# A decoder trunk on one Trainium2 core: two output projection units share one PSUM region inside the last pair of heads

## The chip, the core and the metric

The kernel runs on one core of a Trainium2 chip. The engines of a core work at the same time and wait for each other by semaphores: TensorE (matmuls, PE in the profile; PEld is its loading of weights), VectorE (DVE), ScalarE (ACT), GpSimd (POOL) and SyncE (SP), which here only issues DMAs. The metric is the device time of one launch in microseconds.

## The reference

A step of a decoder trunk with two layers, D = 1024, in float32. A prompt of 1024 tokens and 8 sequences of 4 sample tokens go through it with shared weights.

```python
for layer in range(2):
    xn = rms_norm(h, g_mix[layer])
    if layer == 0:  y = conv_mixers(xn)          # projection, two gated convolutions, output projection
    else:                                        # 16 heads of 64
        q, k, v = qkv_split(xn, w_qkv)
        y = dilated_attention(q, k, v) @ w_o     # three dilated windows, merged; cache for the samples
    h = h + y
    h = h + conv_ffn(rms_norm(h, g_ffn[layer]))  # gate and up, convolution of width 3, silu, down
y = rms_norm(h, g_final)
```

The change touches the product with `w_o` of layer 1: the attention output (1056 tokens by 1024 channels) times a matrix of 1024 by 1024, added to h. Results are y, the new convolution states and the new key and value caches.

## The kernel before, in words

**Layout.** Activations are held transposed: 128 channels on the partitions, the 1056 tokens (1024 of the prompt, 32 samples) along the row, eight such rows of a tile for 1024 channels. A matmul takes 352 tokens, so three make a row. To keep float32 accuracy each operand is split into a high and a low part: `w_sp` holds both parts of a weight unit, `xs` those of the activations. A product is made of three: high by high, high by low, low by high. One weight unit (128 by 1024 numbers, 512 KB) gives 128 output channels. It has eight parts, one for each row of 128 input channels, and a part is 3 x 3 = 9 matmuls.

**Weight stream.** Units follow each other through three slots: SyncE loads into `w_raw` (`load_unit`), ScalarE writes the high part (`split_hi`, line 375), GpSimd the low part (`split_lo`, line 380, counted in `w_lo`). Units 118 to 125 are the output projection (`U_WO` = 118).

**PSUM.** Two regions `reg[0]` and `reg[1]` of three banks, and `ob` of two. Outside attention, units go into the regions in turn. `open_use` lets TensorE write a region once VectorE has emptied it, and `add_to_h` (line 1505) adds a finished region to a row of h. In the attention `reg[1]` holds scores and transposes, and `reg[0]` (`dense`) the projections that run as filling.

**Attention.** The 16 heads are taken in eight pairs. A pair has eight steps s, one for each block of 128 queries, the longest first: step 0 has eight key blocks, step 7 has one. A step's scores go through PSUM to VectorE (adding of the bias and minimum, `neg_scores`, line 1801), ScalarE (exponential), VectorE (normalising, line 1817), TensorE (transposes, `turn`, line 900), copies to `pT` by VectorE (line 1824, head 0) and ScalarE (line 1255, head 1), and TensorE (`weigh`, line 915, probabilities by values). Steps 0 to 3 have more than four key blocks: there `turn(s, 0)` is followed by a second set, `turn(s, 4)`. In steps 0, 1, 3, 5 and 7 a phase of the samples' attention is put in (`sample_phase`), for which SyncE loads the cached keys and values into `kvr`.

**Filling.** TensorE's order is written out by hand. `filler(n)` has 24 places in a pair, n = 0 to 23. In step s, place 3s + 1 stands ahead of the next step's scores and of `turn(s, 0)`, and place 3s + 2 behind `turn(s, 0)` (in step 7 ahead of it). In pairs 0 to 6 each place takes one part of the next pair's q, k or v unit (line 879). In the last pair there is no next one; there places 4, 7, 10, 13, 16, 19 and 22 take parts 0 to 6 of unit 118 (`in_proj`, line 612). A part k needs row k of the attention output split: ScalarE's high part (`att_hi`, line 1260; two rows at the end of steps 0, 1 and 2, one in step 3) and GpSimd's low part (line 1453, counted in `x_lo`). Row 7 is that of the last pair itself; ScalarE and VectorE make it behind the pair (lines 1337 and 1903).

**Behind the pairs.** TensorE waits for the copies of the last samples' output, then runs parts 0 to 6 of unit 119 in region 1, part 7 of unit 118, part 7 of unit 119, and then units 120 to 125. So 81 matmuls stand ahead of unit 120. SyncE loads rows 0 to 2 of h back from HBM once the last sample phase is through (h and `kvr` share memory, line 560), then unit 120 once the last pair's sample output is copied, then rows 3 to 7 (line 566), the FFN state and unit 121. Unit 120's slot shares memory with tiles of the attention, so its load is not earlier.

`VT` is the tile of the pair's value rows before they are turned, 1056 numbers per partition. After its transposes at the start of the pair and its store to HBM it is not used any more in the last pair. The kernel's addresses show that it does not overlap h.

Of the kernel before, what the change touches and what calls it, by code (L numbers as in the profile page):

```python
# [24 lines left out]
ALU = mybir.AluOpType  # L25
# [3 lines left out]
P = 128  # L29
D = 1024  # L30
KD = D // P
# [3 lines left out]
NT, TS = 3, T // 3  # L35
# [7 lines left out]
NPAIR = NH // 2  # L43
# [91 lines left out]
NTA = _n + 1  # L135

KV_LEN = (512, NKEY - 512)

SQ0 = {0: 0, "ln": 8, 1: 12, 2: 20, 3: 28, 4: 36}

# [6 lines left out]
def cnt(u):  # L147

    return u + 1 if u < U_WO else u + 1 - QKV_LATER
# [24 lines left out]
def build(nc, xT, wstream, par, ident_d, ones_d, stA, stB, stF, kva, kvb, wtab, sbias, cache_k, cache_v,  # L174
# [3 lines left out]
    with ExitStack() as ctx:  # L178
# [4 lines left out]
        def sem(name):  # L183
            return ctx.enter_context(nc.semaphore(name))
# [89 lines left out]
        def region(use):  # L274
            return reg[use % 2][:, :, 0:TS]

        def tok(ap):
            return ap.rearrange("p (s t) -> p s t", s=NT)
# [41 lines left out]
        ta_full, ta_free, tb_full, tb_free = (sem(s) for s in ("ta_full", "ta_free", "tb_full", "tb_free"))  # L320
        pv_ok, o_free = sem("pv_ok"), sem("o_free")
        seam_ok = sem("seam_ok")
        sp_neg, sp_exp, sp_ok, so_ok, zero_ok = (sem(s) for s in ("sp_neg", "sp_exp", "sp_ok", "so_ok", "zero_ok"))
        v_chain, a_chain, g_chain = sem("v_chain"), sem("a_chain"), sem("g_chain")

# [264 lines left out]
        def _(pe):  # L590
# [5 lines left out]
            def in_proj(u, r, i=None, ustep=12, rstep=24, x_at=None, order=range(KD), part=range(KD), midway=None,  # L596
                        released=0):


                pe.wait_ge(w_lo, at(cnt(u), i, ustep))  # L600
                open_use(r, i, rstep)
                out = region(r)
                w = w_sp[:, u % 3]
                for n in part:
                    k = order[n]
                    if midway and n == KD // 2:
                        midway()
                    if x_at is not None:
                        pe.wait_ge(x_lo, x_at + n + 1)
                    for wh, xh in ((0, 0), (0, 1), (1, 0)):  # L610
                        for t in range(NT):
                            mm = nc.tensor.matmul(out[:, t, :], w[:, wh, k * P:(k + 1) * P],  # L612
                                                  xs[:, xh, k, t * TS:(t + 1) * TS],
                                                  start=(n == 0 and wh + xh == 0), stop=(n == KD - 1 and wh == 1))
                    if n < released:
                        mm.then_inc(x_free, 1)
                if KD - 1 in part:
                    mm.then_inc(full, 1)
# [233 lines left out]
            def scores(pr, s, c):  # L852
# [7 lines left out]
                                          KT[pr.par][rows, lo:lo + w], start=True, stop=True)  # L860
                mm.then_inc(sc_full, 1)

            def pair(pr):
                k_t = KT[pr.par]

                def filler(n):

                    if pr.last:
                        if n % 3 == 1 and n > 1:
                            in_proj(U_WO, R1, x_at=4 * KD, part=(n // 3 - 1,))  # L870
                        return
                    x, k = divmod(n, KD)
                    if k == 0:
                        pe.wait_ge(aw_lo, pr.n(x + 1, 3))
                        pe.wait_ge(d_free, pr.n(x + 3, 3))
                    w = w_sp[:, pr.slot(x)]
                    for wh, xh in ((0, 0), (0, 1), (1, 0)):
                        for t in range(NT):
                            mm = nc.tensor.matmul(dense[:, t, :], w[:, wh, k * P:(k + 1) * P],  # L879
                                                  xs[:, xh, k, t * TS:(t + 1) * TS],  # L880
                                                  start=(k == 0 and wh + xh == 0), stop=(k == KD - 1 and wh == 1))
                    if k == KD - 1:
                        mm.then_inc(d_full, 1)
# [134 lines left out]
            pairs(pair)  # L1018

            pe.wait_ge(ta_free, NTA * NPAIR + 1)  # L1020
            in_proj(U_WO + 1, FIRST[U_WO + 1], part=range(KD - 1))
            in_proj(U_WO, FIRST[U_WO], x_at=4 * KD, part=(KD - 1,))
            in_proj(U_WO + 1, FIRST[U_WO + 1], part=(KD - 1,))
            for m in range(2, KD - 2):
                in_proj(U_WO + m, FIRST[U_WO + m])
            last_two(U_WO + KD - 2, FIRST[U_WO + KD - 2])
# [439 lines left out]
        def _(dve):  # L1466
# [342 lines left out]
            def pair(pr):  # L1809
# [31 lines left out]
                for s in range(STEPS):  # L1841
# [12 lines left out]
                    if s == 2 and not pr.last:  # L1854
                        dve.wait_ge(d_full, pr.n(4, 3))
                        project(0, dense, QT[1 - pr.par])
                    if s == 4:
                        dve.wait_ge(sp_exp, pr.n(1, 1))
                        chain(nc.vector.reciprocal(snm[:, 4:5], snm[:, 3:4]))
                        nc.vector.tensor_scalar(sps[:, :], sps[:, :], snm[:, 4:5], None, ALU.mult).then_inc(sp_ok, 1)  # L1860
# [44 lines left out]
            dve.wait_ge(o_free, 2 * NPAIR + 1)  # L1905
            chain(nc.vector.memset(g3[:, 0:PAD], 0.0))
            dve.wait_ge(h_back, 16 * 3)
            for m in range(KD):
                if m == 3:
                    dve.wait_ge(h_rest, 16 * (KD - 3))  # L1910
                if m == KD - 2:
                    for x in range(KD - 2):
                        gain_lo(3, 5, x)
                add_to_h(FIRST[U_WO + m], m)
# [171 lines left out]
```

## Time and profile before

| what | value |
|---|---|
| median of 3 runs | 2684.63 us (2684.56 to 2685.1) |
| profiled execution, its own time | 2685.45 us |
| its span | 2683.6 us |
| TensorE busy | 2629.0 us, 98% |
| VectorE / ScalarE / GpSimd busy | 1392.3 / 626.4 / 683.0 us |
| the chain that ended last | TensorE 93%, VectorE 4%, ScalarE 1% |

The span is what the profiler saw from the first to the last instruction; the time of the execution holds a little more around it. Busy time of matmuls overlaps with the loading of their weights. The chain of waits is followed back from the last instruction: each link is the work that the next one waited for. In the views of busy time by stage a row gives the stretch from the span's start and its length, then the busy time of TensorE, its loading of weights, VectorE, ScalarE and GpSimd, each with the number of instructions, then TensorE's granted clock (1.00 is full speed), the mean busy share of the DMA engines and what they moved in GB/s. In a timeline, brackets give how long the engine sat idle before the row and what ended that. All rows below lie between 1659 and 1835 us of the span: pair 6 begins its scores near 1659, the last pair runs from 1736.5 to 1805.7, and the output projection follows.

### The profile page before, as it was taken

Reading aid. Unit: us, or ns where it says so; the run is one execution under the profiler, and the core shown is the slowest. Engines: PE = TensorE matmul, PEld = TensorE weight load, DVE = VectorE, ACT = ScalarE, POOL = GpSimd, SP = SyncE. Lnnn points to the kernel's source line nnn. Section 1 sums busy time; section 2 is a strip of 40 time slices with the busy share of each in tenths; the row PEclk is TensorE's granted clock in tenths of the full one; section 3 lists DMA queues with packets and bytes.
Section 4 is the critical chain, followed back from the end, with each engine's and each line's share of the span. In section 5 each row is a group of like instructions: output and inputs, shape, how many; then the busy total and the mean of one; then the engine's idle time right before and its main releaser. Section 6 shows DMA issues by size and latency. Waiting matters only on the chain.

```text
span 2683.6 us, 41415 instructions
## 1 busy us (share of the span) xinstructions
PE 2629.0 (98%) x17588; PEld 2468.5 (92%) x17588; DVE 1392.3 (52%) x2030; ACT 626.4 (23%) x940; POOL 683.0 (25%) x397
## 2 busy tenths in 40 slices
PE   8999999999999999999999999989999999999997
PEld 8889999999999999997777777769999999999997
DVE  6989855444444444465655555561544444444444
ACT  5110342111111111143333333342311111111112
POOL 1001143332223223340101101124432333323332
PEclk9999999999999999999999999999999999999998
DMA  4101112243333344144444354437444444444411
GB/s 140 48 32 40 48 45 54 63 149 110 110 110 104 108 142 140 50 153 138 145 142 167 133 173 142 163 126 288 166 172 157 157 157 152 169 172 173 172 44 65
DMA packets 93864, 336.72 MB, mean 125 GB/s; under 512 B 22528, under 2 KB 39808, under 8 KB 91136
## 3 DMA queue, kind: packets, MB, share of 16 engines
q1 hardware_dynamic: 93696, 334.20, 36.1%
q8 instruction: 139, 2.28, 0.4%
q14 instruction: 29, 0.24, 0.0%
HBM read 315.88 MB, written 152.25 MB: 174 GB/s over the span
## 4 chain that ended last, share of the span: by engine, by line
PE 93%; DVE 4%; ACT 1%; issue 1%; DMA 0%; POOL 0%; POOLq 0%; DVEq 0%; SPq 0%; ACTq 0%
PE reg L612 49%; PE reg L663 19%; PE reg L879 9%; PE reg L859 3%; PE reg L751 3%; PE ob L915 3%; PE reg L900 1%; PE reg L832 1%; PE ob L725 1%; PE ob L900 1%; PE reg L968 1%; PE reg L632 1%; PE reg L955 1%; DVE neg_s L1801 1%; DVE neg_s L1817 1%
## 5 line engine op out<-in xcount | busy, mean ns | idle before, releaser
L612 PE MATMUL reg<-xs,w_sp 128*128 128x352 f32 x8208 | 1338.7, 324 | 12.1 <-DVE xs L1494 11.7
L612 PEld LDWEIGHTS reg<-xs,w_sp 128*128 128x128 f32 x8208 | 1329.3, 188 | 17.3 <-issue 16.7
L380 POOL TENSOR_TENSOR w_sp<-w_raw,w_sp 128x1024 fp32r<-128x1024 f32 x152 | 370.3, 2436 | 985.4 <-ACT w_sp L375 984.1
L663 PE MATMUL reg<-hid,w_sp 128*128 128x352 f32 x3150 | 511.5, 323 | 0.0
L663 PEld LDWEIGHTS reg<-hid,w_sp 128*128 128x128 f32 x3150 | 508.5, 188 | 0.2 <-DVE tmp L1739 0.2
L375 ACT ACTIVATE w_sp<-w_raw 128x1024 fp32r<-128x1024 f32 x172 | 182.2, 1059 | 1102.8 <-PE reg L612 668.8
L1505 DVE TENSOR_TENSOR h<-reg,h 128x1056 f32<-128x1056 f32 x199 | 250.1, 1257 | 290.5 <-PE reg L663 233.0
L879 PE MATMUL reg<-xs,w_sp 128*128 128x352 f32 x1512 | 279.6, 332 | 0.0
L1705 DVE TENSOR_TENSOR g<-reg,rst 128x1056 f32<-128x1056 f32 x44 | 55.4, 1259 | 415.1 <-PE reg L612 415.1
L879 PEld LDWEIGHTS reg<-xs,w_sp 128*128 128x128 f32 x1512 | 240.6, 188 | 17.7 <-issue 17.6
L398 POOL TENSOR_TENSOR w_sp<-w_raw,w_sp 128x1024 fp32r<-128x1024 f32 x21 | 49.9, 2376 | 477.2 <-ACT w_sp L393 457.9
L1421 POOL TENSOR_TENSOR sil<-sil,rst 128x1056 f32<-128x1056 f32 x44 | 90.4, 2054 | 218.0 <-ACT sil L1192 218.0
L1739 DVE TENSOR_TENSOR tmp<-reg,sil 128x1056 f32<-128x1056 f32 x44 | 55.3, 1257 | 151.2 <-POOL sil L1421 79.6
L1192 ACT ACTIVATE sil<-acc 128x1056 f32<-128x1056 f32 x44 | 47.9, 1089 | 342.9 <-DVE acc L1730 342.9
L1255 ACT ACTIVATE pT<-ob 128x512 f32<-128x512 f32 (+1 forms) x96 | 47.1, 491 | 329.3 <-PE ob L900 329.3
L1718 DVE SCALAR_TENSOR_TENSOR acc<-g,pt,acc 128x1024 f32<-128x1024 f32 x88 | 113.0, 1284 | 12.0 <-DVE acc L1716 1.5
L1801 DVE CUSTOM_DVE_ANT_0 neg_s<-reg,wt 128x512 f32<-128x512 f32 (+1 forms) x192 | 107.2, 558 | 6.6
L1248 ACT ACTIVATE neg_s<-neg_s,nmx 128x896 f32<-128x896 f32 (+7 forms) x128 | 98.1, 768 | 36.8 <-DVE nmx L1806 34.2
L1548 DVE SCALAR_TENSOR_TENSOR g<-g,pt,g 128x1024 f32<-128x1024 f32 x75 | 103.4, 1379 | 2.0
L1824 DVE COPY pT<-reg 128x512 f32<-128x512 f32 (+1 forms) x96 | 53.3, 556 | 97.9 <-PE reg L900 97.5
L1694 DVE TENSOR_TENSOR hid<-tmp,hid 128x1056 fp32r<-128x1056 f32 x44 | 100.3, 2280 | 2.3 <-ACT hid L1195 2.3
L751 PE MATMUL reg<-xs,w_sp 128*128 128x352 f32 x576 | 96.9, 328 | 1.0 <-DVE xs L1501 0.7
(207 smaller groups left out, 1951.7 us busy)
## 6 DMA issues: line engine op xcount, KB each, us to landing
w_raw<-in_wstream SPq DMA_DIRECT2D x193, 512.0 KB, 3.6
out_sv<-in_cache_v SPq DMA_DIRECT2D x16, 4088.0 KB, 15.4
out_sk<-in_cache_k SPq DMA_DIRECT2D x16, 4088.0 KB, 15.1
kvr<-in_kva SPq DMA_DIRECT2D x16, 2048.0 KB, 9.4
kvr<-in_kvb SPq DMA_DIRECT2D x16, 1536.0 KB, 7.0
wt<-in_wtab SPq DMA_DIRECT2D x16, 512.0 KB, 5.6
h<-in_xT SPq DMA_DIRECT2D x4, 1056.0 KB, 11.2
h_spill<-h SPq DMA_DIRECT2D x8, 528.0 KB, 2.6
```

The source lines that it names most:

```text
L375: nc.scalar.activation(w_sp[:, u % 3, 0, :], w_raw[:, u % 3, :], ACT.Copy).then_inc(w_hi, 1)
L380: nc.gpsimd.tensor_tensor(w_sp[:, u % 3, 1, :], w_raw[:, u % 3, :], w_sp[:, u % 3, 0, :].bitcast(F32), ALU.subtract).then_inc(w_lo, 1)
L612: mm = nc.tensor.matmul(out[:, t, :], w[:, wh, k * P:(k + 1) * P], xs[:, xh, k, t * TS:(t + 1) * TS], start=(n == 0 and wh + xh == 0), sto ...
L663: mm = nc.tensor.matmul(out[:, t, :], w[:, wh, kk * 512 + m * P:kk * 512 + (m + 1) * P], hid[:, par_g, kk, xh, t * TS:(t + 1) * TS], start ...
L751: mm = nc.tensor.matmul(out[:, t, :], w[:, wh, (2 * k + m2) * P:(2 * k + m2 + 1) * P], xs[:, xh, place + k, t * TS:(t + 1) * TS], start=(k ...
L879: mm = nc.tensor.matmul(dense[:, t, :], w[:, wh, k * P:(k + 1) * P], xs[:, xh, k, t * TS:(t + 1) * TS], start=(k == 0 and wh + xh == 0), s ...
L1248: nc.scalar.activation(neg_s[:, hh, 0:w], neg_s[:, hh, 0:w], ACT.Exp, bias=nmx[:, m, hh:hh + 1], scale=-1.0, accum_out=lsum[:, 0, hh:hh + ...
L1505: nc.vector.tensor_tensor(tok(h[:, m, :]), region(r), tok(h[:, m, :]), ALU.add).then_inc(free, 1)
L1548: ins = nc.vector.scalar_tensor_tensor(out=y, in0=src, scalar=w, in1=y, op0=ALU.mult, op1=ALU.add)
L1694: nc.vector.tensor_tensor(hid[:, g % 2, c, 1, :], tmp[:, :], hid[:, g % 2, c, 0, :].bitcast(F32), ALU.subtract).then_inc(hid_lo, 1)
L1718: chain(nc.vector.scalar_tensor_tensor(out=y, in0=src, scalar=w, in1=y, op0=ALU.mult, op1=ALU.add))
L1801: nc.vector.tensor_tensor_reduce(out=neg_s[:, hh, lo:lo + w], in0=S[hh][:, 0:w], in1=wt[:, hh, t0:t0 + w], scale=-1.0, scalar=3.0e38, op0= ...
```

## The change

In the last pair the filling now holds twelve parts. Places 4, 5, 7, 8, 10, 11 and 13 take parts 0 to 6 of unit 119 (`part_proj`), into `dense`. VectorE copies that partial sum of seven parts to `VT` in step 4, behind the normalising and ahead of the rescaling of the samples' probabilities. Places 14, 16, 17, 19 and 20 then take parts 0 to 4 of unit 118 into the same region; the first of them waits for the copy. Places 2 and 22 are empty.

Behind the pairs TensorE runs parts 5 to 7 of unit 118, and part 7 of unit 119 alone in region 1: 36 matmuls ahead of unit 120. VectorE adds `VT` to row 1 of h ahead of its first `add_to_h`. What SyncE, ScalarE and GpSimd issue is the same as before and in the same order.

```diff
--- before.py
+++ after.py
@@ -135,6 +135,9 @@
 NTA = _n + 1
 
 KV_LEN = (512, NKEY - 512)
+
+WO_PART = {n: k for k, n in enumerate((4, 5, 7, 8, 10, 11, 13))}
+WO_REST = {n: k for k, n in enumerate((14, 16, 17, 19, 20))}
 
 SQ0 = {0: 0, "ln": 8, 1: 12, 2: 20, 3: 28, 4: 36}
 
@@ -320,6 +323,7 @@
         ta_full, ta_free, tb_full, tb_free = (sem(s) for s in ("ta_full", "ta_free", "tb_full", "tb_free"))
         pv_ok, o_free = sem("pv_ok"), sem("o_free")
         seam_ok = sem("seam_ok")
+        part_full, part_out, part_in = (sem(s) for s in ("part_full", "part_out", "part_in"))
         sp_neg, sp_exp, sp_ok, so_ok, zero_ok = (sem(s) for s in ("sp_neg", "sp_exp", "sp_ok", "so_ok", "zero_ok"))
         v_chain, a_chain, g_chain = sem("v_chain"), sem("a_chain"), sem("g_chain")
 
@@ -860,14 +864,31 @@
                                           KT[pr.par][rows, lo:lo + w], start=True, stop=True)
                 mm.then_inc(sc_full, 1)
 
+            def part_proj(k):
+
+                pe.wait_ge(w_lo, cnt(U_WO + 1))
+                pe.wait_ge(x_lo, 4 * KD + k + 1)
+                w = w_sp[:, (U_WO + 1) % 3]
+                for wh, xh in ((0, 0), (0, 1), (1, 0)):
+                    for t in range(NT):
+                        mm = nc.tensor.matmul(dense[:, t, :], w[:, wh, k * P:(k + 1) * P],
+                                              xs[:, xh, k, t * TS:(t + 1) * TS],
+                                              start=(k == 0 and wh + xh == 0), stop=(k == KD - 2 and wh == 1))
+                if k == KD - 2:
+                    mm.then_inc(part_full, 1)
+
             def pair(pr):
                 k_t = KT[pr.par]
 
                 def filler(n):
 
                     if pr.last:
-                        if n % 3 == 1 and n > 1:
-                            in_proj(U_WO, R1, x_at=4 * KD, part=(n // 3 - 1,))
+                        if n in WO_PART:
+                            part_proj(WO_PART[n])
+                        elif n in WO_REST:
+                            if WO_REST[n] == 0:
+                                pe.wait_ge(part_out, 1)
+                            in_proj(U_WO, R1, x_at=4 * KD, part=(WO_REST[n],))
                         return
                     x, k = divmod(n, KD)
                     if k == 0:
@@ -1018,9 +1039,14 @@
             pairs(pair)
 
             pe.wait_ge(ta_free, NTA * NPAIR + 1)
-            in_proj(U_WO + 1, FIRST[U_WO + 1], part=range(KD - 1))
-            in_proj(U_WO, FIRST[U_WO], x_at=4 * KD, part=(KD - 1,))
-            in_proj(U_WO + 1, FIRST[U_WO + 1], part=(KD - 1,))
+            in_proj(U_WO, FIRST[U_WO], x_at=4 * KD, part=range(len(WO_REST), KD))
+            u = U_WO + 1
+            open_use(FIRST[u])
+            for wh, xh in ((0, 0), (0, 1), (1, 0)):
+                for t in range(NT):
+                    mm = nc.tensor.matmul(region(FIRST[u])[:, t, :], w_sp[:, u % 3, wh, (KD - 1) * P:KD * P],
+                                          xs[:, xh, KD - 1, t * TS:(t + 1) * TS], start=(wh + xh == 0), stop=(wh == 1))
+            mm.then_inc(full, 1)
             for m in range(2, KD - 2):
                 in_proj(U_WO + m, FIRST[U_WO + m])
             last_two(U_WO + KD - 2, FIRST[U_WO + KD - 2])
@@ -1854,6 +1880,10 @@
                     if s == 2 and not pr.last:
                         dve.wait_ge(d_full, pr.n(4, 3))
                         project(0, dense, QT[1 - pr.par])
+                    if s == 4 and pr.last:
+                        dve.wait_ge(part_full, 1)
+                        dve.wait_ge(vt_out, 16 * NPAIR)
+                        nc.vector.tensor_copy(tok(VT[:, :]), dense).then_inc(part_out, 1)
                     if s == 4:
                         dve.wait_ge(sp_exp, pr.n(1, 1))
                         chain(nc.vector.reciprocal(snm[:, 4:5], snm[:, 3:4]))
@@ -1905,6 +1935,9 @@
             dve.wait_ge(o_free, 2 * NPAIR + 1)
             chain(nc.vector.memset(g3[:, 0:PAD], 0.0))
             dve.wait_ge(h_back, 16 * 3)
+            dve.wait_ge(part_out, 1)
+            nc.vector.tensor_tensor(h[:, 1, :], VT[:, :], h[:, 1, :], ALU.add).then_inc(part_in, 1)
+            dve.wait_ge(part_in, 1)
             for m in range(KD):
                 if m == 3:
                     dve.wait_ge(h_rest, 16 * (KD - 3))
```

## Rows read from the trace of the kernel before

**Rows 1.** Busy time by stage: pair 6, then the last pair with its tail.

```profile
1659.08:1736.50 77.42, 76.26 (x663) 59.52 (x663) 44.07 (x140) 26.53 (x66) 7.12 (x3) 1.00 0.43 149
1736.50:1807.00 70.50, 57.15 (x524) 38.20 (x525) 46.46 (x139) 32.58 (x70) 20.29 (x8) 0.98 0.38 131
```

**Rows 2.** Chain of waits from the last pair on: start us, us, what.

```profile
1759.22 0.49 ACT pT L1255
1759.71 1.94 ACT xs L1260 x2
...
1763.74 2.60 DVE neg_s L1817
...
1802.08 0.35 PE reg L974 x8
...
1805.67 11.94 PE reg L612 x72
...
1819.21 30.81 PE reg L612 x189
```

**Rows 3.** Timeline of GpSimd: start us, us, line, operation, count, idle before.

```profile
1760.76 5.15 POOL L1453 TENSOR_TENSOR xs<-att,xs 128x1056 fp32r<-128x1056 f32 x2 [6.29 <-ACT xs L1260]
...
1781.38 2.45 POOL L1453 TENSOR_TENSOR xs<-att,xs 128x1056 fp32r<-128x1056 f32 x1 [6.67 <-ACT xs L1260]
1812.49 2.40 POOL L380 TENSOR_TENSOR w_sp<-w_raw,w_sp 128x1024 fp32r<-128x1024 f32 x1 [28.66 <-ACT w_sp L375]
```

**Rows 4.** Timeline of TensorE in the last pair, steps 1, 4, 5 and 6.

```profile
1757.35 0.60 PE L900 MATMUL ob<-ident,neg_s 128*128 128x128 f32 x4
1758.29 0.55 PE L900 MATMUL reg<-ident,neg_s 128*128 128x128 f32 x3 [0.35 <-DVE pT L1824]
...
1781.31 1.74 PE L612 MATMUL reg<-xs,w_sp 128*128 128x352 f32 x9
...
1786.69 1.09 PE L915 MATMUL ob<-pT,vrow 128*64 128x128 f32 x16 [1.27 <-ACT att L1267]
...
1789.67 1.95 PE L968 MATMUL reg<-kvr,spT 128*32 128x128 f32 x64 [0.86 <-ACT spT L1284]
...
1795.37 0.88 PE L915 MATMUL ob<-pT,vrow 128*64 128x128 f32 x12 [0.67 <-ACT pT L1255]
...
1799.49 0.66 PE L915 MATMUL ob<-pT,vrow 128*64 128x128 f32 x8 [0.56 <-ACT pT L1255]
```

**Rows 5.** Timeline of ScalarE: a row's conversion, and two splits of weights.

```profile
1780.23 1.07 ACT L1260 ACTIVATE xs<-att 128x1056 fp32r<-128x1056 f32 x1
...
1811.35 1.06 ACT L375 ACTIVATE w_sp<-w_raw 128x1024 fp32r<-128x1024 f32 x1 [3.99 <-DMA w_raw<-in_wstream]
1819.49 1.06 ACT L375 ACTIVATE w_sp<-w_raw 128x1024 fp32r<-128x1024 f32 x1 [7.08 <-DMA w_raw<-in_wstream]
```

**Rows 6.** Timeline of VectorE: copies of two sizes, and a subtraction.

```profile
1757.55 0.69 DVE L1824 COPY pT<-reg 128x512 f32<-128x512 f32 x1 [1.81 <-PE reg L900]
...
1804.23 0.29 DVE L1824 COPY pT<-reg 128x128 f32<-128x128 f32 x1 [1.31 <-PE reg L900]
1807.39 1.26 DVE L1903 TENSOR_TENSOR xs<-att,xs 128x1056 fp32r<-128x1056 f32 x1 [2.88 <-ACT xs L1337]
```

**Rows 7.** Timeline of SyncE's queue: issues, not landings.

```profile
1737.80 0.34 SPq L526 DMA_DIRECT2D out_vT<-VT  x1
...
1802.54 1.29 SPq L560 DMA_DIRECT2D h<-h_spill  x3
1805.65 0.33 SPq L368 DMA_DIRECT2D w_raw<-in_wstream  x1
```

**Rows 8.** The loads of h from line 560, issue to landing.

```profile
DMA to landing us min/median/max: 3.8/4.7/5.5
```

**Rows 9.** Busy time, granted clock and DMA, columns as in rows 1.

```profile
1769.00:1773.00 4.00, 4.00 (x40) 2.78 (x42) 2.73 (x13) 3.15 (x6) 3.37 (x2) 0.57 0.00 0
1807.00:1811.00 4.00, 4.00 (x27) 4.00 (x26) 1.30 (x2) 0.36 (x1) 0.00 (x0) 1.00 1.03 415
```


## The prediction

> **What bounds the kernel now.** TensorE is the bound nearly everywhere, so I first compared two stretches in the view of busy time by stage. The reader is to see there that pair 6 takes 77.42 us with TensorE busy for 76.26 us, while the last pair (1736.50 to 1807.00) takes 70.50 us with TensorE busy for only 57.15 us [rows 1]. So 13.35 us of TensorE time lie idle in the last pair, and that is what more filling could use. Then I read the chain of waits of the last pair. It shows whether this idle time is free. It is mostly not: between two steps the chain runs from the second set of transposes of a step to ScalarE's copy of them (1759.22), to two conversions of attention rows (1759.71, 1.94 us), and on to VectorE's normalising, whose second instruction takes 2.60 us (1763.74) [rows 2]. GpSimd shows why that one is so long: its two subtractions run from 1760.76 to 1765.91, and VectorE ends 0.43 us behind them [rows 2, 3]. So the idle gaps of TensorE are links of a chain that TensorE itself starts; what delays the transposes delays all of it. Last I read what follows the pair: 81 matmuls without a pause (72 of them 11.94 us, so a part of nine costs 1.49 us), one addition by VectorE, and from 1819.21 the third projection unit, whose matmuls then run on unbroken [rows 2].
>
> **The change part by part.**
>
> *Moved work.* The number of projection matmuls stays the same. The last pair had seven parts and gets twelve; behind the pair nine parts become four. Behind the pair 5 x 1.49 = 7.5 us leave TensorE's queue. Inside it, six parts are added between the transposes of a step and what comes next (numbers 5, 8, 11, 14, 17, 20), and the one at number 22 goes. Number 22 stood behind the last sample phase, so up to the end of that phase, which I call S (1802.45 before, where the matmuls that start at 1802.08 end [rows 2]), six parts are added. What decides is how late S becomes.
>
> *Steps 1 to 3.* Here the new part stands between the first and the second set of transposes. In step 1 the first set is through at 1757.9, the second started at 1758.29 after an idle 0.35 us [rows 4]. Now it starts at about 1759.4: +1.1. Everything behind it in the chain, the conversions, GpSimd's subtractions and the normalising that ends with them, moves as much. In step 2 the idle time ahead of the second set is near nothing, and the part ahead of the scores (number 7) now needs row 2, which GpSimd has ready 2.6 us after it starts (half of 5.15 us, 1760.76) [rows 3]; this wait ends as late as the normalising lets the transposes go anyway and adds 0.1 to 0.2. Step 2: +1.25. Step 3 has the same idle time of 0.35 us ahead of its second set (there are two such rows): +1.15. Together +3.5 us by ScalarE's copy at the end of step 3. These are between 0 (all in idle time) and 1.5 each; I take the sum of the single steps because the chain names every link.
>
> *Step 4.* The part at number 13 was the fourth one and needed a row long done; it becomes the seventh and needs row 6. ScalarE makes it at 1780.23 and GpSimd subtracts from 1781.38 for 2.45 us, to 1783.83 [rows 3, 5], while TensorE is ready for the part at 1781.31 [rows 4]. With the +3.5 on the rows and +2.4 on TensorE, TensorE waits some 3.5 us, and the part ends at 1788.8. Scores and transposes are behind it in TensorE's queue, and they end at 1790.8, 5.5 us later than before. VectorE's new copy (1056 columns from PSUM; a copy of 512 takes 0.69 us, one of 128 some 0.29, so about 1.26 us by the slope, and not under 0.69) stands ahead of the sample rescaling, of the transposes' copy and of the next scores, which all wait for it [rows 6]. It ends at 1790.2, so the other unit can open the region without a wait at number 14. That part takes 1.5 us of a gap of 1.27 us (1786.69) [rows 4], and the sample's transposes and their copies come 5.7 us later than before (1789.67, where TensorE waited 0.86 us) [rows 4]. The wait for the values' store costs nothing: it was issued at 1737.80, some 50 us earlier [rows 7].
>
> *Steps 5 and 6.* The new part falls into the gaps of 0.67 us and 0.56 us ahead of the weighing (1795.37 and 1799.49) [rows 4]: +0.85 and +0.95. S comes 7.5 us late, about 1810.0. All six parts are 9.0 us, so only 1.5 us of them lie in idle time, or rather in that and in what the two stalls leave. Lower bound +1 (all but one part hidden), upper +10.
>
> *Behind S.* Before, the third unit started at S + 16.76. Now TensorE has transposes, the last weighing and four parts, 36 matmuls or 6.0 us: without the part at number 22 it gets to the four parts at S + 1.9 (before at S + 3.2), and is through at S + 8.0. The last row's conversion ends on VectorE some 3.0 us after the end of the weighing, since ScalarE's copies and the 1.26 us subtraction (1807.39) follow each other [rows 6]; the first two parts (2.98 us) just cover it. The new addition of the stored sum (two inputs in SBUF, as the subtraction of 1.26 us [rows 6]) needs rows of h that were asked for at S + 0.1 and landed within 5.5 us of each issue [rows 7, 8], that is by S + 6.5, and is done at S + 7.7. It delays the first addition by 1.2 us but not TensorE, for what comes next is later.
>
> *The new wait.* The third unit's weights are not moved by the change. SyncE issued their load at 1805.65, once the pair had ended, behind three loads of h; they landed by 1811.35, ScalarE took 1.06 us and GpSimd 2.40 us from 1812.49, so that they were ready at 1814.89, S + 12.45 [rows 3, 5, 7]. Before, 4.3 us of matmuls still lay over this. Now TensorE is done at S + 8.0 and stands for some 4.2 us. The load is issued 1.3 us earlier against S; but its queue is full (DMA share 1.03, 415 GB/s) [rows 9], and three times 528 KB lie ahead, so between 0 and 1.3 us of it come through; I take 0.3, near the full queue.
>
> *The sum.* S +7.5; start of the third unit S + 12.15 instead of S + 16.76, so -4.6; together +2.9, rounded to +3.0 us. Behind that nothing changes: the next weights landed at about S + 17 (1819.49) and their split ends 3.5 us later, at about S + 20.6 [rows 5], while TensorE wants them at S + 12.15 + 11.8 = S + 24; the rest of h is wanted later still. The profiled execution took 2685.45 us, its span 2683.6 us; so 2688.5 us for such an execution, and since the median of the runs is 0.8 us lower, 2687.6 us.
>
> **The rivals.**
>
> *A, the clock falls in the new waits.* The trace shows it once: from 1769 to 1773 the granted clock was 0.57 in the mean, so nearly all of it at the 1.2 GHz level (0.5), after a stretch in which TensorE often paused; in before it lay beside VectorE's work and cost nothing [rows 9]. Over full matmuls such a dip costs 4 x (1 - 0.57) = 1.7 us. The change makes two longer pauses, 3.5 us in step 4 and 4.2 us ahead of the third unit; with a dip behind each, +6.4 us, 2691.0 us, which is slower. It decides from the point where both dips come, or one and a longer S. Against it: the mean clock of the last pair is 0.98 with all its gaps of up to 1.3 us [rows 1, 4], and more filling makes the pair denser. The Trainium skill (TensorE: Matmul & The Clock Gate, Part 1) has a rule that speaks against this change: the clock is cut after a stretch without activity and comes back only after a busy one. By that rule both dips are likely; the trace neither shows nor excludes it for such lengths.
>
> *B, the parts fit the gaps.* The idle 13.35 us are more than the 9.0 us added [rows 1]. If the steps' gaps give way, S comes only 2 us late (the stall in step 4), and the sum is 2 - 4.6 = -2.6: 2682.0 us. For it: pair 6 runs 24 parts in 77.42 us. Against it: pair 6 has no conversions of rows, and the chain of the last pair names ScalarE and VectorE right behind the transposes [rows 2]. Break-even is S at +4.6.
>
> *C, the change does all it can.* Parts hidden and weights there in time: -7.5 us, 2677.1 us. It needs the load earlier than it is issued; nothing moves it.
>
> **How the numbers follow.** Forecast 62%, A 18%, B 17%, C 3%. Two thirds of A reach past 0.2% (5.4 us, about what a measurement of this kernel can tell from no change), of B hardly anything, C all: faster 4%, slower 12%, same 84%. The range reaches from B's nearer half to just past A's value: 2682.5 to 2691.5 us.
>
> **What would show it.** Right: in the chain the transposes of steps 1 to 3 come 1.1 to 1.3 us later per step; the seventh part waits for GpSimd's seventh subtraction; the last sample phase ends about 7.5 us later; ahead of the third unit TensorE waits about 4 us for GpSimd's split. Wrong: if S moves by under 4.6 us, or if that last wait is under 2 us, the sign is wrong. A granted clock of 0.5 in the first part of the third unit would be rival A.

## The result, and the profile after

The changed kernel took 2689.31 us (median of 19 runs, 2688.58 to 2691.65), the kernel before 2685.04 us (19 runs, 2683.83 to 2688.23) beside it. The ratio is 1.0017, with a 95% interval of 1.0011 to 1.0023: 4.6 us slower, 3.0 to 6.2 (the medians alone differ by 4.3). The forecast was 3.0 us slower. The profiled execution has a span of 2687.6 us, 4.0 more than before.

Single spans differ by more than a microsecond in stretches that no kernel here changes: the last pair began 1.12 us earlier than in the profile of before (1735.28 instead of 1736.40). So I measure from T, the start of the last pair's first scores (1736.40 before), to S, the end of its last sample phase, from S to the start of unit 120, and the length of the first four units from there (288 matmuls). This table holds all profiles, in us; each value is a difference of starts and ends in the chain of waits and in TensorE's timeline. "By profile" is the sum against that of before; "by runs" is the difference of the medians, each kernel against before in the same comparison. The two differ by up to 2 us, for one profile is one execution.

| kernel | T to S | S to unit 120 | four units | sum | by profile | by runs |
|---|---|---|---|---|---|---|
| before | 66.03 | 16.78 | 46.84 | 129.65 | | |
| after | 75.17 | 11.43 | 48.39 | 134.99 | +5.3 | +4.3 |
| e1_early_load | 75.12 | 9.63 | 46.84 | 131.59 | +1.9 | +1.2 |
| e2_before_early_load | 66.03 | 16.77 | 46.84 | 129.64 | 0.0 | +0.3 |
| e3_warm | 73.62 | 11.28 | 46.88 | 131.78 | +2.1 | +3.7 |
| e4_row_ready | 72.64 | 11.16 | 49.59 | 133.39 | +3.7 | +3.2 |
| e5_more_early | 69.58 | 16.76 | 46.84 | 133.18 | +3.5 | +3.7 |
| e6_more_late | 67.56 | 16.75 | 46.84 | 131.15 | +1.5 | +2.5 |
| e7_six | 70.04 | 11.40 | 49.47 | 130.91 | +1.3 | +2.2 |
| e8_six_early | 69.94 | 8.27 | 46.84 | 125.05 | -4.6 | -2.7 |
| e9_two_in_step1 | 69.53 | 8.27 | 46.84 | 124.64 | -5.0 | -3.6 |
| e10_six_early_again | 70.04 | 8.25 | 46.84 | 125.13 | -4.5 | -2.6 |

The forecast's terms were 73.5, 12.15 and 46.84. The first came 1.7 us too long, the second 0.7 us better, the third 1.55 us too long.

The view of busy time by stage, columns as in [rows 1], for pair 6 and for the last pair of the changed kernel:

```profile
1659.00:1735.40 76.40, 75.24 (x661) 59.27 (x661) 43.11 (x141) 26.54 (x66) 7.14 (x3) 1.00 0.42 148
1735.40:1812.00 76.60, 63.03 (x561) 45.34 (x561) 48.11 (x140) 30.84 (x67) 20.27 (x8) 0.96 0.32 106
```

TensorE stands idle for 13.6 us of the last row, as much as the 13.35 before: old gaps were filled, but new waits arose, and the pair became longer. (The stretch of [rows 1] ended 1.3 us into the matmuls behind the pair, this one 0.3 us ahead of them; the idle time is not touched by that.) The mean granted clock is 0.96, where it was 0.98.

The chain of waits (start, length, what) answers to [rows 2]:

```profile
1758.99 0.49 ACT pT L1281
...
1760.53 2.44 POOL xs L1479
...
1763.10 1.68 PE reg L874 x9
...
1768.78 0.38 ACT pT L1281
...
1781.86 0.28 ACT pT L1281
...
1784.23 2.42 POOL xs L1479
...
1786.78 1.92 PE reg L874 x9
...
1810.10 0.40 PE reg L995 x8
...
1812.27 6.06 DMA w_raw<-in_wstream
...
1818.35 1.06 ACT w_sp L379
...
1819.49 2.36 POOL w_sp L384
...
1821.88 28.16 PE reg L616 x163
```

In it the reader sees three things. In step 2 and in step 4 the chain runs through GpSimd's subtraction (1760.53 and 1784.23) into a part of the projection (1763.10 and 1786.78): TensorE waits for a row of attention. And ahead of unit 120 (1821.88) it runs over a DMA, ScalarE and GpSimd; before, 72 matmuls stood in that place.

TensorE's timeline, with the idle time in brackets, answers to [rows 4]:

```profile
1756.58 1.71 PE L874 MATMUL reg<-xs,w_sp 128*128 128x352 f32 x9
1758.13 0.49 PE L921 MATMUL reg<-ident,neg_s 128*128 128x128 f32 x3
...
1786.78 1.92 PE L874 MATMUL reg<-xs,w_sp 128*128 128x352 f32 x9 [3.19 <-POOL xs L1479]
...
1791.64 1.70 PE L616 MATMUL reg<-xs,w_sp 128*128 128x352 f32 x9
...
1793.28 1.09 PE L936 MATMUL ob<-pT,vrow 128*64 128x128 f32 x16
...
1796.17 1.95 PE L989 MATMUL reg<-kvr,spT 128*32 128x128 f32 x64 [0.78 <-ACT spT L1310]
...
1802.60 0.88 PE L936 MATMUL ob<-pT,vrow 128*64 128x128 f32 x12
...
1807.51 0.66 PE L936 MATMUL ob<-pT,vrow 128*64 128x128 f32 x8
```

The new part at 1756.58 used up the 0.35 us ahead of the second transposes and pushed them by 1.0 us against T. Part 13 waits 3.19 us (1786.78). The gaps of 1.27, 0.67 and 0.56 us ahead of the weighing are gone (1793.28, 1802.60, 1807.51). The 0.78 us ahead of the sample's values (1796.17) stayed.

VectorE's timeline shows the new copy, what stands behind it, and the new addition:

```profile
1788.74 1.26 DVE L1886 COPY VT<-reg 128x1056 f32<-128x1056 f32 x1 [1.23 <-PE reg L874]
...
1791.37 0.69 DVE L1850 COPY pT<-reg 128x512 f32<-128x512 f32 x1 [0.56 <-PE reg L921]
...
1817.16 1.26 DVE L1939 TENSOR_TENSOR h<-VT,h 128x1056 f32<-128x1056 f32 x1 [1.84 <-issue]
1818.45 2.62 DVE L1531 TENSOR_TENSOR h<-reg,h 128x1056 f32<-128x1056 f32 x2
```

The copy took 1.26 us, as the slope had it. The transposes' copy at 1791.37 then waited 0.56 us for TensorE, so the new copy was not what ended last there. SyncE's queue, to be held against [rows 7]:

```profile
1810.57 1.29 SPq L564 DMA_DIRECT2D h<-h_spill  x3
1812.27 0.33 SPq L372 DMA_DIRECT2D w_raw<-in_wstream  x1
```

The load of unit 120's weights is issued 1.70 us behind the loads of h, and not 3.11 us. It landed by 1818.35, S + 7.9, where before it was S + 8.9.

Last the granted clock, the figure ahead of the last two in each row, in the steps 3 and 4 and at the start of unit 120:

```profile
1776.00:1780.00 4.00, 3.59 (x16) 2.83 (x17) 1.96 (x6) 0.60 (x1) 0.00 (x0) 0.72 0.98 367
1780.00:1784.00 4.00, 3.13 (x29) 2.67 (x27) 1.13 (x6) 2.14 (x4) 0.00 (x0) 0.85 0.06 19
1784.00:1788.00 4.00, 1.22 (x8) 1.25 (x9) 2.49 (x4) 1.56 (x5) 2.41 (x1) 1.00 0.00 0
1788.00:1792.00 4.00, 4.00 (x17) 2.54 (x17) 2.66 (x5) 0.07 (x1) 0.00 (x0) 0.57 0.00 0
1822.00:1825.00 3.00, 3.00 (x11) 3.00 (x12) 0.00 (x0) 0.00 (x0) 0.00 (x0) 0.53 1.03 416
1825.00:1828.00 3.00, 3.00 (x18) 3.00 (x18) 0.00 (x0) 1.43 (x2) 0.30 (x1) 0.90 1.42 600
```

A dip is a stretch in which the granted clock lies near 0.5, the 1.2 GHz level. Three dips lie over work that counts: one in step 3 (the first two rows), one in step 4 from 1788 on, behind the wait of part 13, and one at the very start of unit 120. The last is what made the four units 1.55 us longer. The one in step 4 can be sized by the time from the start of part 13 to the start of the part at place 14: 4.86 us here (1786.78 to 1791.64), and 3.56 us at full clock (e8_six_early, shown with that experiment), so about 1.3 us, an estimate. The one in step 3 is sized with e3_warm.

### The profile page after: what moved, and what is told of

It is laid out like the page before. It is cut to its first block, busy times and chain, and to the rows that moved or that the text cites. A ratio compares the mean times of both kernels' runs of the same rounds, so it can differ in the third digit from the quotient of the medians.

```text
span 2687.6 us, 41423 instructions
## 1 busy us (share of the span) xinstructions
PE 2629.2 (98%) x17588; PEld 2469.8 (92%) x17588; DVE 1395.5 (52%) x2032; ACT 626.1 (23%) x940; POOL 683.0 (25%) x397
## 4 chain that ended last, share of the span: by engine, by line
PE 93%; DVE 4%; issue 1%; ACT 1%; DMA 0%; POOL 0%; POOLq 0%; DVEq 0%; SPq 0%; ACTq 0%
PE reg L616 49%; PE reg L667 19%; PE reg L900 9%; PE reg L863 3%; PE reg L755 3%; PE ob L936 2%; PE reg L921 1%; PE reg L836 1%; PE ob L729 1%; PE ob L921 1%; PE reg L989 1%; PE reg L636 1%; PE reg L976 1%; DVE neg_s L1827 1%; DVE neg_s L1843 1%
```

## The experiments

All twelve profiles are read against their own T. The ratios are those of the runs, each with its 95% interval; five rounds resolve about 2.4 us either way, so the steps are told apart by the profiles, and the runs say whether the whole follows.

**The weights of unit 120 earlier.** In the changed kernel (e1_early_load) and in the kernel before (e2_before_early_load) the load is issued in step 4 of the last pair, into half of the bias table that nobody reads from there on; the splits read it from there, and the FFN state, which shares that memory, is loaded behind the split.

```diff
                 if not pr.last:
                     sp.wait_ge(sc_free, pr.n(2 * CHUNK0[4] + 1, 2 * NCH))
                     load_table(0, wtab[0][pr.p + 1])
+                else:
+                    sp.wait_ge(sc_free, pr.n(2 * CHUNK0[4] + 1, 2 * NCH))
+                    sp.dma_start(wt[:, :, 0:512], wstream[U_WO + 2]...).then_inc(w_in[(U_WO + 2) % 3], 16)
...
-            load_unit(sp, U_WO + 2, (U_WO + 2) % 3)
```

> The changed kernel with the weights of unit 120 loaded during step 4 of the last pair, into the first half of the bias table, which is free from there on; nothing is left out. My theory: TensorE's wait of 3.4 us for these weights goes; what is late next is VectorE's addition to h (the stored sum is added first, up to S + 7.9, then unit 118's region is emptied at about S + 9.3), so unit 120 starts some 2 us earlier against S, and the clock dip behind the wait (1.55 us) goes too: 3.5 us faster than the changed kernel, about +0.8 us against before. Rival 'it is all the longer pair' (the wait only takes up slack): no change, +4.3 us against before. Rival 'the wait is all of it': -0.5 us against before or less.

Measured: ratio 1.0003 (0.9994 to 1.0012), 2685.76 us where before took 2684.58: +1.2 us by the medians. The wait for the weights is gone, the four units are back at 46.84 us, and what stands ahead of unit 120 is VectorE's addition of the stored sum and the first addition behind it, as expected. VectorE's timeline, then TensorE's:

```profile
1816.36 1.54 DVE L1948 TENSOR_TENSOR h<-VT,h 128x1056 f32<-128x1056 f32 x1 [1.79 <-issue]
```

```profile
1819.34 15.92 PE L620 MATMUL reg<-xs,w_sp 128*128 128x352 f32 x97 [1.60 <-DVE h L1540]
```

Unit 120 waits 1.60 us for VectorE, and no dip follows that shorter pause. The sum in the profiles fell by 3.4 us (expected 3.5).

> The kernel before with the same earlier load of unit 120; nothing is left out. My theory: there 81 matmuls cover the load and its split, so it gives nothing: within 0.3 us of before. A rival in which the queue behind the load (rows of h, unit 121) matters would show 1 us or more, faster.

Measured: ratio 0.9999 (0.9990 to 1.0008), and in the profile every term as before. The load was covered there. The two runs together show that the changed kernel made the wait, by moving the matmuls that had hidden it.

**Work in the wait.** e3_warm keeps the changed kernel and puts 20 matmuls that nobody reads into the wait.

```diff
             mm.then_inc(full, 1)
+            for t in range(20):
+                nc.tensor.matmul(ob[:, 0, 0:TS], xs[:, 0, KD - 1, 0:P], xs[:, 0, KD - 1, 0:TS], start=True, stop=True)
             for m in range(2, KD - 2):
```

> The changed kernel with 20 matmuls of 352 columns that nobody reads, put into the wait ahead of unit 120 (some 3.3 us of the 3.4 us). My theory: the granted clock falls to the 1.2 GHz level in the first part of unit 120 because TensorE stood still ahead of it; with work there the dip goes and unit 120 still starts when its weights are ready: 1.5 us faster than the changed kernel, +2.8 us against before, and a clock of 1.00 in the first 5 us of unit 120. Rival (the dip is chance or comes from elsewhere): dip stays, +4.3 to +4.6 us.

Measured: ratio 1.0011 (1.0002 to 1.0020), +3.7 us by the medians, between the +2.8 expected and the rival's +4.3, so the runs don't decide. The profile bears out the theory: the filling ends as the weights are ready, and the clock stays whole.

```profile
1817.28 3.36 PE L1051 MATMUL ob<-xs 128*128 128x352 f32 x20
1820.66 9.65 PE L616 MATMUL reg<-xs,w_sp 128*128 128x352 f32 x58
```

```profile
1776.00:1780.00 4.00, 3.08 (x19) 2.33 (x20) 2.28 (x8) 0.60 (x1) 0.00 (x0) 1.00 1.02 373
1784.00:1788.00 4.00, 2.27 (x9) 2.21 (x9) 2.39 (x4) 0.50 (x2) 1.59 (x1) 0.77 0.00 0
1788.00:1792.00 4.00, 4.00 (x23) 2.75 (x21) 3.49 (x9) 1.13 (x3) 0.00 (x0) 0.81 0.01 2
1820.66:1825.00 4.34, 4.34 (x27) 4.34 (x28) 0.00 (x0) 0.00 (x0) 0.00 (x0) 1.00 1.03 419
```

The last row of the view is the start of unit 120, at 1.00, and the four units took 46.88 us in place of 48.39. In the three profiles with a wait of 3.1 to 3.4 us and nothing in it (after, e4_row_ready, e7_six) they took 48.39, 49.59 and 49.47. The other rows show two things more. The pair's code is the same here as in the changed kernel, but step 3 ran without a dip (1776 to 1780 at 1.00 instead of 0.72), and T to S is 1.55 us shorter. And the dip behind the wait of part 13 came here too (the rows from 1784 and 1788; part 13 took 2.63 us in place of about 1.7), as it did in after and e1_early_load:

```profile
1785.73 2.63 PE L874 MATMUL reg<-xs,w_sp 128*128 128x352 f32 x9 [3.20 <-POOL xs L1482]
```

**Part 13 without its wait.** e4_row_ready takes row 5 in place of row 6 in the seventh part.

```diff
+                row = 5 if k == 6 else k
-                pe.wait_ge(x_lo, 4 * KD + k + 1)
+                pe.wait_ge(x_lo, 4 * KD + row + 1)
...
-                                              xs[:, xh, k, t * TS:(t + 1) * TS],
+                                              xs[:, xh, row, t * TS:(t + 1) * TS],
```

> The changed kernel, but the part at place 13 takes attention row 5 in place of row 6, which is long ready (so the output projection's unit 119 is computed from row 5 twice). My theory: TensorE's wait of 3.2 us for GpSimd's seventh subtraction goes, but VectorE's normalising and the copy stand behind it, so the sample phase of step 5 comes only about 2 us earlier, and the whole is 2.0 us faster than the changed kernel, +2.3 us against before. Rival (wait fully hidden beside the normalising): no change. Rival (wait counts in full): -3.2 us, +1.1 us against before.

Measured: ratio 1.0008 (0.9999 to 1.0017), +3.2 us by the medians; T to S is 2.5 us shorter than in the changed kernel (expected 2.0). TensorE's timeline:

```profile
1783.21 1.72 PE L875 MATMUL reg<-xs,w_sp 128*128 128x352 f32 x9
...
1786.70 0.66 PE L922 MATMUL reg<-ident,neg_s 128*128 128x128 f32 x4 [0.93 <-DVE neg_s L1844]
...
1788.46 1.71 PE L616 MATMUL reg<-xs,w_sp 128*128 128x352 f32 x9 [0.51 <-DVE VT L1887]
...
1793.36 1.95 PE L990 MATMUL reg<-kvr,spT 128*32 128x128 f32 x64 [1.15 <-DVE spT L1894]
```

Part 13 starts at once (1783.21). The transposes then wait 0.93 us for the normalising and the first part of unit 118 waits 0.51 us for VectorE's new copy, which had stayed hidden behind the wait. So the wait of 3.19 us was worth 2.5 us in this profile. About 1.3 us of that is the dip behind the wait: the clock was 1.00 from 1784 to 1792 here and fell to 0.57 in the changed kernel. Both profiles have the dip of step 3. The wait by itself was thus worth some 1.2 us, for the other two waits take its place.

**More parts in the kernel before.** Three further parts, with nothing taken away behind the pair: at places 5, 8, 11 (e5_more_early) or 14, 17, 20 (e6_more_late).

```diff
+                        elif n in (5, 8, 11):
+                            w = w_sp[:, U_WO % 3]
+                            for wh, xh in ((0, 0), (0, 1), (1, 0)):
+                                for t in range(NT):
+                                    nc.tensor.matmul(dense[:, t, :], w[:, wh, 0:P], xs[:, xh, 0, t * TS:(t + 1) * TS],
+                                                     start=False, stop=False)
```

> The kernel before with three more parts, at places 5, 8 and 11 (behind the first transposes of steps 1 to 3); each multiplies row 0 by unit 118's weights once more, so unit 118's output is wrong. Nothing is taken away behind the pair. My theory: each costs 0.8 to 1.25 us of its 1.49, since ScalarE, GpSimd and VectorE wait for the second transposes: +3.0 us against before, +4.3 us if the dip of the clock comes to lie over work that counts. Rival 'the pair has 13 us of idle TensorE time, parts fit in it': 0. Rival 'each counts in full': +4.5 us.

> The kernel before with three more parts, at places 14, 17 and 20 (ahead of the weighing in steps 4 to 6), again row 0 by unit 118 once more, so unit 118's output is wrong. My theory: the gaps there were 1.27, 0.67 and 0.56 us, so the parts cost 0.2, 0.85 and 0.95 us: +2.0 us against before. Rival 'parts fit': 0; rival 'in full': +4.5 us.

Measured: 1.0013 (1.0004 to 1.0022) for the early places, 1.0007 (0.9998 to 1.0016) for the late ones. In the profiles T to S grew by 3.55 and 1.53 us, of 4.5 us of matmuls each; no other term moved. By the medians it was 3.7 and 2.5 us; these cannot tell either value from the expectations, so the profiles carry what follows. The 3.55 us of the early places hold a dip. The weighing of step 4 started 2.29 us late against T (1787.73 here with T at 1735.15; 1786.69 before), and then the clock fell to 0.57 (1788 to 1792): the weighing took 1.57 us in place of 1.09, and the samples' values behind it started 3.56 us late (1791.98).

```profile
1787.73 1.57 PE L921 MATMUL ob<-pT,vrow 128*64 128x128 f32 x16 [1.27 <-ACT att L1273]
...
1791.98 1.96 PE L974 MATMUL reg<-kvr,spT 128*32 128x128 f32 x64 [0.78 <-ACT spT L1290]
```

So the early places cost 2.3 us, or 0.77 us a part, and the dip 1.27 us; the late ones, with the dip where it lay before (1769 to 1773), 0.51 us a part. The rival by which parts fit into the pair's idle time falls for both, and so does that of the full cost. Against the 0.2 + 0.85 + 0.95 us that I had for the late places, they were 0.5 us cheaper.

**Six and six.** e7_six puts six parts of each unit into the pair, takes VectorE's copy to the start of step 4, and so frees part 13 of its late row. e8_six_early adds the earlier load and moves the addition of the stored sum behind the first addition to h. e10_six_early_again is the same kernel run again.

```diff
-WO_PART = {n: k for k, n in enumerate((4, 5, 7, 8, 10, 11, 13))}
-WO_REST = {n: k for k, n in enumerate((14, 16, 17, 19, 20))}
+WO_PART = {n: k for k, n in enumerate((4, 5, 7, 8, 10, 11))}
+WO_REST = {n: k for k, n in enumerate((13, 14, 16, 17, 19, 20))}
...
+                    if s == 4 and pr.last:
+                        dve.wait_ge(part_full, 1)
+                        dve.wait_ge(vt_out, 16 * NPAIR)
+                        nc.vector.tensor_copy(tok(VT[:, :]), dense).then_inc(part_out, 1)
                     for hh in range(2):
                         norm(s, hh)
```

> The changed kernel arranged otherwise: six parts of unit 119 (places 4, 5, 7, 8, 10, 11), VectorE's copy at the start of step 4, where VectorE waits for ScalarE anyway, then six parts of unit 118 (places 13, 14, 16, 17, 19, 20); behind the pair again 36 matmuls. Nothing is left out. My theory: the wait of step 4 and the copy's cost go, so the last sample phase is 4.9 us later than before instead of 9.2; the wait for unit 120's weights and the dip behind it stay: 4.9 - 5.4 + 1.55 = +1.0 us against before, 3.3 us faster than the changed kernel. Rival 'step 4 cost nothing of its own': +4.3 us.

> The arrangement of six and six parts, with unit 120's weights loaded in step 4 as in the run of the earlier load, and VectorE's addition of the stored sum moved behind its first addition to h. Nothing is left out. My theory: TensorE goes from the 36 matmuls straight into unit 120, at S + 8.0 in place of S + 16.8 before, with S 4.9 us later and no wait for the clock to fall in: 3.9 us faster than before (2680.7 us where before takes 2684.6), 2.9 us faster with a dip inside the pair. If the sums are wrong and the longer pair takes all back, 0 or slower.

> The same kernel as the six and six arrangement with the earlier load, once more, on the same chip as the run beside it: 2.7 to 3.9 us faster than before.

Measured: e7_six 1.0005 (0.9996 to 1.0014); its profile gives +1.3 us, with S 4.0 us later than before instead of 9.1, the wait for the weights as in the changed kernel, and the dip behind it (49.47 us, 2.6 more than at full clock where I had expected 1.55). Of the 5.1 us that S moved against the changed kernel, some 2.9 are the two dips of steps 3 and 4, which this profile doesn't have; the expectation, which knew nothing of them, named 4.3 for the wait and the copy. e8_six_early 0.9989 (0.9980 to 0.9998), 2682.15 us where before took 2684.83, and the same ratio and interval again in e10_six_early_again. That is 2.7 and 2.6 us faster, below the 3.9 expected. The profiles give 4.6 and 4.5 us, without a dip between T and unit 120; they are of executions 3.1 and 1.4 us faster than the medians of their kernels, so it may be that others have dips, which no profile here shows. Both are faster than the two given kernels. TensorE goes into unit 120 with 0.15 us between the matmuls' modelled end and its start, and the only wait of step 4 worth a line is that for the normalising:

```profile
1781.15 1.71 PE L621 MATMUL reg<-xs,w_sp 128*128 128x352 f32 x9
...
1784.64 0.66 PE L926 MATMUL reg<-ident,neg_s 128*128 128x128 f32 x4 [0.93 <-DVE neg_s L1862]
...
1785.64 1.71 PE L621 MATMUL reg<-xs,w_sp 128*128 128x352 f32 x9
...
1810.97 1.62 PE L1053 MATMUL reg<-xs,w_sp 128*128 128x352 f32 x9
1812.74 27.58 PE L621 MATMUL reg<-xs,w_sp 128*128 128x352 f32 x169
```

From the start of part 13 (1781.15) to that of the part at place 14 (1785.64) it takes 4.49 us; without the 0.93 us of waiting that is 3.56 us, the value used above for the dip of step 4.

**Where in a step.** e9_two_in_step1 moves the second part of step 1 from behind the first transposes to behind the first part.

```diff
-                        if n in WO_PART:
+                        if n == 4:
+                            part_proj(0)
+                            part_proj(1)
+                        elif n in WO_PART and n > 5:
                             part_proj(WO_PART[n])
```

> The arrangement of six and six parts with the earlier load, with the second part moved from place 5 (between the two sets of transposes of step 1) to place 4, behind the first one, where TensorE waited 1.5 us for VectorE. Nothing is left out. My theory: behind the first transposes the part cost 1.0 us; at the new place it fits except for 0.3 us, because row 1 is subtracted only just then: 0.7 us faster than the same kernel without the move, in the time from the last pair's first scores to unit 120 (78.2 us there, 77.5 us expected); too little to be told by the runs' times. Rival 'a part costs the same wherever it stands': no difference.

Measured: 0.9986 (0.9977 to 0.9995), 2681.45 us where before took 2685.07. The stretch from T to unit 120 is 77.8 us against 78.2 and 78.3 in the two profiles without the move: 0.4 to 0.5 us of the 0.7 expected. The runs cannot tell it from e8_six_early. The part waits 0.34 us for row 1 and delays the scores behind it by 0.44 us against T, since they had stood behind a wait of 1.54 us:

```profile
1752.16 1.71 PE L879 MATMUL reg<-xs,w_sp 128*128 128x352 f32 x9
1754.22 1.70 PE L879 MATMUL reg<-xs,w_sp 128*128 128x352 f32 x9 [0.34 <-POOL xs L1498]
1755.85 1.13 PE L868 MATMUL reg<-KT,QT 64*128 64x512 f32 x4
```

## Why the prediction was right

**How late the pair runs.** This table gives, against T and in us, when ScalarE's copy behind the second transposes started in steps 1, 2 and 3, when the weighing of step 4 and the samples' values of step 5 started, and when S came. The first row holds the times of before, the others how much later each came.

| kernel | step 1 | step 2 | step 3 | weighing 4 | values | S | dips before S |
|---|---|---|---|---|---|---|---|
| before | 22.82 | 31.80 | 42.60 | 50.29 | 53.27 | 66.03 | step 2 to 3, costs nothing |
| after | +0.89 | +1.70 | +3.98 | +7.71 | +7.62 | +9.14 | steps 3 and 4 |
| e3_warm | +0.88 | +1.72 | +2.43 | +6.16 | +6.07 | +7.59 | step 4 |
| e4_row_ready | +0.86 | +1.68 | +3.94 | +4.81 | +5.09 | +6.61 | step 3 |
| e5_more_early | +0.86 | +1.63 | +2.31 | +2.29 | +3.56 | +3.55 | behind weighing 4 |
| e8_six_early | +0.86 | +1.68 | +2.35 | +2.46 | +2.38 | +3.91 | none |

The copies of before behind steps 2 and 3, in its chain of waits:

```profile
1768.20 0.38 ACT pT L1255
...
1779.00 0.28 ACT pT L1255
```

**Steps 1 to 3.** Expected +3.5 us by the end of step 3. Without a dip it was 2.3 to 2.4 us (e3_warm, e5_more_early, e8_six_early): 0.9, 0.8 and 0.7 us by step, where I had 1.1, 1.25 and 1.15. The chain through the transposes was read rightly, but its sum was 1.1 us too large. In the changed kernel ScalarE's copy at the end of step 3 came 4.0 us late, for a clock dip in step 3, which the forecast had not placed there, put 1.55 us on top.

**Step 4.** The wait for row 6 was foreseen at 3.5 us and was 3.19 us. That removing it would not give all of it back, because the normalising and the copy stand behind, is what e4_row_ready showed. The dip behind it was rival A's, not the forecast's.

**Steps 5 and 6.** In the changed kernel S came 1.5 us later than the sample phase of step 5 (7.6 us late against T, S 9.1), with 1.8 expected. Together with step 4's part the same places cost only 1.5 us when nothing else was added.

**S as a whole** was 9.1 us late in the profile, 7.5 expected. Less the dips of step 3 (1.55 us) and step 4 (about 1.3 us) it would be some 6.3 us, an estimate. The 7.6 us of e3_warm look like a hit, but they hold one dip, which made up for a sum that was too large: that is luck. That the dip of step 3 is the cause of its 1.55 us rests on a comparison of profiles (after and e1_early_load with it at 75.17 and 75.12 us, e3_warm without it at 73.62), not on an experiment.

**The wait for unit 120's weights** is the heart of the forecast and held: 3.4 us of standing still, seen in the chain and removed by e1_early_load. The load was issued 1.4 us earlier against S and 1.1 us of it came through, where I had 0.3 of 1.3; the queue was less of a limit than I took it for, and this made S to unit 120 0.7 us shorter than forecast.

**What is late next.** I had VectorE's new addition end at S + 7.7 and said it costs nothing in this kernel. It ended at S + 8.0, and unit 118's addition at S + 9.3, still ahead of the weights. Once these were early, it set the start of unit 120.

**Rival A.** Its mechanism came whole: it put a dip behind each of the two new waits, and both came. Behind the wait ahead of unit 120 the clock was 0.53, the forecast's own sign of this rival, for 1.55 us, and e3_warm shows that the standing still is what does it. Behind the wait of part 13 a dip of about 1.3 us came in all three profiles that have this wait (after, e1_early_load, e3_warm). The Trainium skill (TensorE: Matmul & The Clock Gate, Part 1) has the clock cut after a stretch without activity. These profiles agree: 3.1 to 3.4 us without matmuls were followed by the 1.2 GHz level in six of six cases, 1.6 us without them ahead of unit 120 (e1_early_load) were not. Such a stretch is not all there is to it, for the dip of step 3 came behind a pause of 1.92 us. My argument against the rival also had a gap missing. The last pair of before pauses for up to 1.54 us, not 1.3:

```profile
1755.79 1.13 PE L859 MATMUL reg<-KT,QT 64*128 64x512 f32 x4 [1.54 <-DVE snm L1834]
```

**The sum.** Without its three dips (1.55, about 1.3 and 1.55 us) the profile's +5.3 us would be +0.9, an estimate, where the forecast had +2.9 without any dip: S 1.2 us and the wait 0.7 us too long. So the 3.0 us forecast and the 4.6 us measured lie near each other because two errors offset: terms 2 us too large, and dips of 4.4 us left out. The path and the waits were right; that the number came so near is luck in part. Rival A, at 6.4 us, had the mechanism, on the same sum that was too large.

**Rival B** (parts fit the gaps) is refuted by e5_more_early and e6_more_late, **rival C** by the wait itself.

## What to carry to other kernels

Idle time of the bounding engine is free only where nobody waits for what stands behind it; count each gap at the wait that ends it, and not the stage's sum. Work that is moved out of a stretch may have been the cover of a load that nobody sees in the profile: look up when each next input is ready and how much of the old work lay over that. A pause of TensorE can cost its own length and then the slower clock behind it: the wait of 3.4 us took 5 us of TensorE's time here, of which the earlier load gave back 3.4, since the next input was late too. When a forecast meets the measured time, check its terms one by one, for errors can offset.

## What was not expected of the hardware

With a part added at each of the places 5, 8 and 11, the dip of the clock that before lay at 1769 to 1773 came at 1776 to 1780 in after, e1_early_load and e4_row_ready (0.72, 0.57 and 0.64), but in e3_warm, e7_six, e8_six_early and e10_six_early_again that stretch ran at 1.00, with the same work up to there. In e5_more_early, where the parts at places 7 and 10 take rows that are ready and do not wait, it came only at 1788. So the same code meets a dip in one execution and not in the next, and T to S of one kernel differed by 1.55 us. In the 8 us ahead of the three dips at 1776 TensorE had been busy for 5.8 to 5.9 us, with pauses of 1.9 us at most; the four profiles without the dip have that pause too (1.93 us in e3_warm). What tells the executions apart stays open.

VectorE's addition of two operands in SBUF took 1.54 us in e1_early_load, where GpSimd's split ran beside its start, and 1.26 us in the changed kernel, where GpSimd stood still.
